# Tile 0's last feed-forward moved under tile 1's expert rows, with each down block as a sum of its own

## The reference, cut to what matters

```python
    u = expert_u[experts]            # (tokens, 8, 16, 1024)
    vsel = expert_v[experts]
    act = gelu(einsum('thkd,td->thk', u, hb))
    x = x + mod5 * einsum('thk,thkd->td', gate * act, vsel)
```

```python
for l in range(2):
    h = rms_norm(x, norm_mix[l])
    x = x + (short_conv_mixer(h) if l == 0 else moba_attention(h, ...))
    x = x + mem_cross_attention(rms_norm(x, ...), memory_l)
    x = x + (silu(g) * u) @ w_down[l]     # g, u = split(rms_norm(x, ...) @ w_gu[l]), 2816 wide each
return rms_norm(x, norm_final)
```

## Time and profile before

| | |
|---|---|
| median of 3 runs | 1847.34 us (1842.53 to 1847.86) |
| the profiled execution's own time | 1849.94 us |
| its span, first to last instruction | 1848.1 us |
| mean granted clock of TensorE | 0.942 of full |
| PE busy, span | 1631.3 us, 88% |
| moved from and to memory | 595.21 MB, 322 GB/s over the span |

### The profile page before, as it was taken

One profiled execution on the slowest core, in us unless ns is written; L12 is line 12 of the kernel. 1 busy time (PEld: TensorE's weight loads), 2 busy tenths in 40 slices (PEclk: granted clock), 3 DMA queues, 4 the chain that ended last, 5 costly groups with the idle time before them and its releaser, 6 DMA issues.

```text
span 1848.1 us, 15547 instructions
## 1 busy us (share of the span) xinstructions
PE 1631.3 (88%) x5460; PEld 760.7 (41%) x5460; DVE 739.3 (40%) x1784; ACT 485.1 (26%) x1267; POOL 284.0 (15%) x268
## 2 busy tenths in 40 slices
PE   6998998497679997987899998889999999988998
PEld 3444464163134542333333333344445444454443
DVE  3653156766594566546544544441101010031000
ACT  3311224322322323324343224232111010122110
POOL 1000002333333333222222223220000000000000
PEclk8998999799789998899999999999999999999999
DMA  9535338999999999999999999977775877654674
GB/s 355 198 144 182 141 136 325 395 388 417 421 386 374 402 421 420 414 421 398 400 397 421 421 420 421 415 321 268 285 284 211 318 289 274 266 222 182 245 300 182
DMA packets 94956, 595.21 MB, mean 322 GB/s; under 512 B 7024, under 2 KB 7024, under 8 KB 28192
## 3 DMA queue, kind: packets, MB, share of 16 engines
q1 hardware_dynamic: 56576, 319.28, 44.2%
q0 software_dynamic: 37584, 270.75, 36.0%
q10 hardware_dynamic: 720, 4.19, 0.6%
HBM read 593.15 MB, written 1.05 MB: 322 GB/s over the span
## 4 chain that ended last, share of the span: by engine, by line
PE 75%; DMA 9%; DVE 8%; ACT 4%; issue 2%; POOL 1%; DVEq 0%; SPq 0%; ACTq 0%; POOLq 0%
PE bank L973 35%; PE bank L1139 9%; PE bank L1052 8%; DMA arena<-in_peer_rows,pidx 7%; PE bank L684 6%; PE bank L946 3%; DVE arena L2063 3%; PE bank L937 2%; DMA ring<-in_w_mod 2%; PE bank L761 2%; PE bank L980 1%; PE bank L738 1%; PE bank L1033 1%; PE bank L781 1%; PE bank L656 1%
## 5 line engine op out<-in xcount | busy, mean ns | idle before, releaser
L1601 POOL DMA_INDIRECT arena<-in_peer_rows,pidx x256 | 279.1, 1090 | 917.6 <-PE bank L1139 596.1
L1139 PE MATMUL bank<-arena,keep 128*32 128x512 f32 x1024 | 279.0, 698 | 124.8 <-ACT keep L1558 124.7
L2063 DVE SCALAR_TENSOR_TENSOR arena<-arena,ring 128x1024 f32<-128x1024 f32 x256 | 305.7, 1223 | 173.0 <-DMA arena<-in_peer_rows,pidx 170.8
L973 PE MATMUL bank<-ring,arena 128*128 128x512 f32 x736 | 322.2, 597 | 9.7 <-ACT arena L1459 7.9
L973 PE MATMUL bank<-ring,hT_all 128*128 128x512 f32 x544 | 241.5, 599 | 4.9 <-DVE hT_all L2120 2.6
L973 PEld LDWEIGHTS bank<-ring,arena 128*128 128x128 f32 x736 | 139.7, 192 | 181.4 <-issue 181.4
L1139 PEld LDWEIGHTS bank<-arena,keep 128*32 128x32 f32 x1024 | 53.0, 120 | 298.0 <-ACT keep L1558 165.7
L973 PEld LDWEIGHTS bank<-ring,hT_all 128*128 128x128 f32 x544 | 102.0, 191 | 136.8 <-issue 136.7
L2170 DVE TENSOR_TENSOR x_all<-x_all,bank 128x512 f32<-128x512 f32 x24 | 16.5, 688 | 228.8 <-PE bank L1052 125.7
L1545 ACT ACTIVATE pf<-pf 128x2 f32<-128x2 f32 x128 | 25.8, 201 | 305.5 <-DVE arena L2063 305.2
L684 PE MATMUL bank<-ring,hT_all 128*128 128x512 f32 x192 | 89.0, 622 | 3.0 <-DVE hT_all L1678 3.0
(11 more groups left out here) (365 smaller groups left out, 1559.0 us busy)
## 6 DMA issues: line engine op xcount, KB each, us to landing
ring<-in_weights SPq DMA_DIRECT2D x126, 2048.0 KB
ring<-in_w_mod SPq DMA_DIRECT2D x12, 2048.0 KB
ring<-in_w_in SPq DMA_DIRECT2D x6, 2048.0 KB
ring<-in_weights SPq DMA_DIRECT2D x8, 1024.0 KB
arena<-in_peer_rows,pidx POOLq DMA_INDIRECT x256
ring<-in_weights SPq DMA_DIRECT2D x8, 512.0 KB
mem_all<-in_b_mod POOLq DMA_DIRECT2D x3, 512.0 KB, 11.0
hT_all<-in_xT ACTq DMA_DIRECT2D x1, 1024.0 KB, 7.3
```

What stands on the lines that cost most here:

```text
L973: m = mm(b[:, :], src[:, k], slot8[w][:, k], start=(k == 0), stop=(k == KC - 1))
L1139: m = mm(acc[b][r:r + 32, :], diag[n % 8], vslot[n % SLOTS][:, b * 512:(b + 1) * 512], start=(n % 128 < 4), stop=(n % 128 >= 124))
L1601: nc.gpsimd.indirect_dma_start(out=row_in[n % SLOTS], out_offset=None, in_=a["peer_rows"], in_offset=bass.IndirectOffsetOnAxis(ap=pidx[:, ...
L2063: stt(uslot[n % SLOTS], uslot[n % SLOTS], 1.0, h2g[n % 4], ALU.mult, ALU.mult, accum_out=pact2[:, 16 * (g % 2) + k:16 * (g % 2) + k + 1]). ...
```

## The change

All of tile 0's steps except `final 0` are placed under the rows; the planner's time for a pick is 5.9 us for 3.7, so that the last step lands at n = 250. `LATE` goes, and `AFTER_ROWS` is `final 0` of tile 0 and then tile 1's steps alone. SP's load order follows, 17 blocks of tile 0's second `gu1` and `dn1` now ahead of tile 1's first. The order of the other steps is the same; their places change. Some of them by n, before and after:

| step | before | after |
|---|---|---|
| turn mem0 / probs0 / values0 | 156 / 166 / 170 | 152 / 160 / 164 |
| turn ffn0 / fturn0 5 / turn blk | 174 / 200 / 212 | 168 / 184 / 192 |
| bprobs / bvalues / turn mem1 | 228 / 232 / 236 | 204 / 208 / 212 |
| probs1 / values1 / mo1 0, 1 | 246 / 250 / 252 | 220 / 224 / 226 |
| turn ffn1 / gu1 0, 1 / dn1 4, 5 | behind the rows | 228 / 230 / 250 |

A down block is now a unit: its contraction starts and ends in its own bank, and VectorE adds it to `x`. This holds for both tiles and layers. Two buffers of tile 0 move: the second layer's attention output and its probabilities.

```diff
-LAYER_FIRST, LAYER_LAST, PICK_US = 136, 252, 3.7
-UNDER_ROWS, LATE = [], []
+LAYER_FIRST, PICK_US = 136, 5.9
+UNDER_ROWS = [_w for _w, _, _ in STEPS]
 _at, _load = LAYER_FIRST, float(LAYER_FIRST)
 for _w, _us, _lag in STEPS:
     _at = max(_at + _lag, 2 * int(_load // 2))
     _load = max(_load, _at) + _us / PICK_US
-    if _at <= LAYER_LAST and not LATE:
-        UNDER_ROWS.append(_w)
+    if _w != "final 0":
+        assert _at < 256
         PICK_WORK.setdefault(_at, []).append("layer 0 " + _w)
-    else:
-        LATE.append((_w, _us))
-AFTER_ROWS = []
-for _w, _us, _lag in STEPS:
-    while _lag and LATE:
-        _late, _late_us = LATE.pop(0)
-        AFTER_ROWS.append((0, _late))
-        if _late_us > 2 and not (_late[:2] == "dn" and _late[-1] not in "25"):
-            break
-    AFTER_ROWS.append((1, _w))
-AFTER_ROWS += [(0, _w) for _w, _ in LATE]
+AFTER_ROWS = [(0, "final 0")] + [(1, _w) for _w, _, _ in STEPS]
...
-                zT=..., cvT=blocks(high), qT=blocks(high), oT=blocks(low),
-                probs=[v.rearrange("p (h n) -> p h n", h=MH) for v in (first, later)], probs_low=work,
+                zT=..., cvT=blocks(high), qT=blocks(high), oT=[blocks(low), blocks(high)],
+                probs=[v.rearrange("p (h n) -> p h n", h=MH) for v in (first, low)], probs_low=work,
...
                 elif kind == "dn":
                     half, c = divmod(int(arg), 3)
-                    if c == 0:
-                        open_unit(f"dn{l}{t}{half}", steps_ahead=True)
-                    b = bank[unit(f"dn{l}{t}{half}") % 4]
                     w = weights(piece[f"dn{l}{t}", int(arg)])
-                    for k in range(8 * c, min(8 * c + 8, FC)):
+                    ks = range(8 * c, min(8 * c + 8, FC))
+                    b = open_unit(f"dn{l}{t}{arg}")
+                    for k in ks:
                         if half == 0 and k % 4 == 0:
                             unit_read(f"ft{l}{t}{k // 4}")
-                        m = mm(b[:, :], v.fT[k], slot8[w][:, k % 8], start=(k == 0), stop=(k == FC - 1))
-                    if c == 2:
-                        open_unit(f"dn{l}{t}{half}", opened_ahead=True)
-                    m.then_inc(unit_ready if c == 2 else sem(f"dn{l}{t}_used"), 1)
+                        m = mm(b[:, :], v.fT[k], slot8[w][:, k % 8], start=(k == ks[0]), stop=(k == ks[-1]))
+                    m.then_inc(unit_ready, 1)
...
-                elif kind in ("cout", "mo", "bo") or kind == "dn" and arg in "25":
-                    half = int(arg) if kind != "dn" else int(arg) // 3
-                    name = {"cout": f"co{t}", "mo": f"lo{l}{t}", "bo": f"bo{t}", "dn": f"dn{l}{t}"}[kind] + str(half)
+                elif kind in ("cout", "mo", "bo", "dn"):
+                    half = int(arg) // (3 if kind == "dn" else 1)
+                    name = {"cout": f"co{t}", "mo": f"lo{l}{t}", "bo": f"bo{t}", "dn": f"dn{l}{t}"}[kind] + arg
                     c = slice(half * 512, (half + 1) * 512)
+                    if kind == "dn" and arg not in "03":
+                        copied(f"dn{l}{t}{int(arg) - 1}")
                     tt(x[:, t, c], x[:, t, c], unit_in(name)[:, :], ALU.add).then_inc(unit_free["D"], 1)
```

More of the change, by code:

```diff
@@ L268, in units_of @@
                  "mo": [("lo{l}{t}{a}", "D")], "gu": [("gu{l}{t}{a}", "D")], "fturn": [("ft{l}{t}{a}", "A")],
-                 "dn": [("dn{l}{t}" + str(int(arg) // 3), "D")] if arg in "25" else [],
[1 row of a table added]
                  "bk": [("bk{t}{a}", "A")], "bq": [("bq{t}{a}", "A")], "bv": [("bv{t}{a}", "A")],
@@ L444, in tile_buffers @@
                 squares=work, hT=blocks(at((hT_all, 1024), (arena, 3072))), kvT=blocks(first), b_tok=low, z_tok=high, q_tok=low,
-                zT=at((h2_all, 0), (arena, 6144), 1040).rearrange("p (k n) -> p k n", k=KC), cvT=blocks(high), qT=blocks(high), oT=blocks(low),
-                probs=[v.rearrange("p (h n) -> p h n", h=MH) for v in (first, later)], probs_low=work,
+                zT=at((h2_all, 0), (arena, 6144), 1040).rearrange("p (k n) -> p k n", k=KC), cvT=blocks(high), qT=blocks(high), oT=[blocks(low), blocks(high)],
+                probs=[v.rearrange("p (h n) -> p h n", h=MH) for v in (first, low)], probs_low=work,
                 pT=work.rearrange("p (h k n) -> p h k n", h=MH, k=2),
@@ L541, in build_program @@
                 last_unit[name, i] = {"cin": "ci", "cout": "co"}.get(step, step) + f"{t}{i}"
[L542 to L545, removed]
+            elif step[:-1] in ("q", "mo", "gu", "dn") and step[-1] in "01":
+                last_unit[name, i] = {"q": "lq", "mo": "lo"}.get(step[:-1], step[:-1]) + f"{step[-1]}{t}{i}"
         def part_read(i):
@@ L563, in wait_released @@
                 eng.wait_ge(unit_ready, unit(last_unit[name, i]) + 1)
-            elif (name, i) in middle:
+            else:
                 eng.wait_ge(sem("piece_used"), middle.index((name, i)) + 1)
-            else:
-                assert name[:2] == "dn"
-                eng.wait_ge(sem(f"{name}_used"), 2 * (i // 3) + i % 3 + 1)
         def tile_x_wait(eng, t, name, u):
@@ L574, in tile_x_wait @@
             else:
-                eng.wait_ge(unit_free["D"], units_freed({"mem0": "co", "ffn0": "lo0", "blk": "dn0", "mem1": "bo", "ffn1": "lo1", "final": "dn1"}[name] + f"{t}{u}", "D"))
+                eng.wait_ge(unit_free["D"], units_freed({"mem0": "co{t}{u}", "ffn0": "lo0{t}{u}", "blk": "dn0{t}{d}", "mem1": "bo{t}{u}", "ffn1": "lo1{t}{u}",
+                                                              "final": "dn1{t}{d}"}[name].format(t=t, u=u, d=3 * u + 2), "D"))
         @block.sync
@@ L1035, in layer_step @@
                 elif kind == "mo":
-                    layer_unit(f"lo{l}{t}{arg}", (f"mo{l}{t}", int(arg)), v.oT, (f"v{l}{t}0", f"v{l}{t}1"))
+                    layer_unit(f"lo{l}{t}{arg}", (f"mo{l}{t}", int(arg)), v.oT[l], (f"v{l}{t}0", f"v{l}{t}1"))
                 elif kind == "gu":
@@ L1498, in layer_step @@
                 elif kind == "values":
-                    unit_copy(f"v{l}{t}1", v.oT[:, 4:8])
+                    unit_copy(f"v{l}{t}1", v.oT[l][:, 4:8])
                 elif kind == "gu":
@@ L2185, in layer_step @@
                 elif kind == "values":
-                    unit_copy(f"v{l}{t}0", v.oT[:, 0:4])
+                    unit_copy(f"v{l}{t}0", v.oT[l][:, 0:4])
                 elif kind == "gu":
```

## The result

The changed kernel takes 1872.37 us in the median (1862.61 to 1873.19, 4 runs) against 1847.33 before: a ratio of 1.0125, 95% interval 1.0102 to 1.0149. It is slower by 25 to 26 us; 17 were forecast, as 1864, with a range of 1836 to 1883.

A forecast was written before the change was run, and what follows sets the result against it. Rows stage before: TensorE and DMA both nearly full, 37 of 53.3 us idle put on VectorE's order. +124.6 under the rows and -107.2 behind give +17.4 on 1847.3: 1864 us, 8 in 10 within 1836 to 1883.

The forecast's parts named there:

- The rows stage: From pair n = 136 to the last pair: grows by 124.6 us as tile 0's last feed-forward moves in.
- the gaps were counted slot by slot: TensorE's waits at ten rows-stage slots, priced from VectorE's evacuation, top-k block and next dots: together 48.3 us.
- The short waits: Rows stage: some ten further TensorE waits of 0.5 to 2 us, together 8.7 us.
- the late-row waits: Rows stage: 16 us of TensorE's idle time before, put on late transfers, goes in the changed kernel.
- The rival that made the change a gain: Rows stage: only transfers count, products fill the gaps, growth is 82.2 us, time down to 1822; chance 0.17.
- Behind the rows: From the last pair to tile 1's feed-forward: 112.8 us for 220.0, a gain of 107.2.
- The first product: Tile 1's convolution start behind the last pair: 9.3 us, waiting for the norm's row, whose load takes 6.9.
- 1.0 for the clock: Behind the rows: 1.0 us added for the clock after the longer gap ahead of tile 1's convolution.
- the memory attention: Tile 1 behind the rows: priced at 44.4 us, turn to turn, from its twin where tile 1 ran alone.
- From tile 1's feed-forward on: The rest of the kernel after tile 1's first steps: nothing changes.
- The partial sums: Down blocks ending in their own banks: 16 more VectorE adds, 11 us, lie under products and cost 0.
- each gap above 3.3 us leaves the next pair slow: Rows stage: the pair after such a gap takes 3.63 us for 1.91; nine for eight, +1 us.

The follow-up runs named there:

- a_again: The changed kernel once more with no edit, on another occasion: 1870.23 us, ratio to before 1.0144.
- a_ahead: The changed kernel with VectorE's dot products taken one pair earlier in its order from n = 136: 1834.65 us, ratio to before 0.9932.
- a_notop: The changed kernel without the top-k blocks of the last six groups of tile 1's picks: 1828.21 us, ratio to before 0.9913.
- a_light: The changed kernel loading only 256 KB of 2 MB of each weight block used under the rows: 1866.16 us, ratio to before 1.0115.
- b_light: The kernel before, loading only 256 KB of 2 MB of each weight block used under the rows: 1821.42 us, ratio 0.9861.
- old_plan: The changed kernel with the step places of before, keeping the separate down blocks and moved buffers: 1845.39 us, ratio to before 0.9990.
- the mixed one: The changed kernel with dots one pair ahead and tile 0's last six down blocks dealt behind the rows: 1821.17 us, ratio to before 0.9869.
- a_ahead4: The changed kernel with dots two pairs ahead and tile 0's final step two places later: 1878.51 us, ratio to before 1.0180.
- b_ahead: The kernel before with VectorE's dot products taken one pair earlier from n = 136: 1843.61 us, ratio 0.9979.

## Why the prediction was right

**The rows stage.** The forecast was +124.6 us; it was +121.7 in the first profile and +124.3 in `a_again`. Of products it had 120.9, measured as 115.9 and 120.2, and of idle time 3.7, measured as 5.9 and 4.1. Inside, the gaps were counted slot by slot, and in the first profile each came within half a microsecond: 160: 7.3, measured 7.00; 192: 5.8 and 5.91; 204: 7.0 and 7.33; 208: 4.9 and 4.48; 220: 6.3 and 5.99; 224: 3.1 and 2.62; 184: 3.7 and 3.88; 152, 168 and 212: 3.4 and 3.36. Sum of the ten 48.3 and 47.3; idle in all 57.0 and 59.2. The short waits were 11.9 us and not 8.7; three were longer than the 2 us I gave them, 2.22 at n = 156, 2.04 at 244 and 2.61 at 252. That the cause is VectorE's order is shown from two sides: `a_ahead` moves the dots and leaves the work, `a_notop` leaves the block out and keeps the order, and both take 34 us off the stage.

**Transfers.** That the late-row waits would go was right (0.8 us left, and `a_light`: no change). Their share in the kernel before was put at 16 us; `b_light` has 21.8, of which 14.4 are idle time (53.3 to 38.9, forecast 37 left) and 7.4 busy time, much of it in products that no longer follow a gap at the lower clock: 32 products at n = 154 took 15.67 us in before and 13.97 in `b_light`. The forecast, +124.6, already took the idle time off. The rival that made the change a gain, stage bound by transfers, is refuted by `a_light`. Its point of decision was well put: gaps below 40 us. `a_ahead` has 32.6 and is faster than before.

**Behind the rows.** The forecast 112.8 us was measured as 112.9 and, in `a_again`, 111.8 (1378.31 to 1490.13), but three of its terms were wrong and cancelled; that the sum fits is luck. The first product came after 6.0 us and not 9.3: I had taken the load's 6.9 us over, and in its new place it took 3.7. The first five blocks took 36.9 us from start to start (1385.97 to 1422.87) and not 34.3, where I had 1.0 for the clock. And the memory attention took 46.0 us (1446.85 to 1492.86) and not its twin's 44.4: its 32 products with the values ran 5.44 us for 3.81.

**Where it was short.** From tile 1's feed-forward on I wrote that nothing changes. It took 378.4 us for 373.7, and 378.2 in `a_again` (1490.13 to 1868.3). 3.4 of it are two starts: the first three blocks after each turn take 22.5 us and not 20.8. Another 1.6 are again 32 products of a memory attention; smaller differences of both signs make the rest. This is the step that was wrong by the most, 4.7 us. The first profile has 3.8 us more ahead of n = 136, which `a_again` doesn't have. Together the spans differ by 23.2 and 20.2 us, where the medians differ by 25 and 26. That difference lies mostly in which executions were profiled: before's was 2.6 us above its median of the first comparison and 5.7 above that of the second, the changed kernel's 0.8 above it and at it.

**The partial sums** were priced at 0, and `old_plan` agrees; the last down projection's 88 products take 37.93 us in before and in the changed kernel.

## What to carry to other kernels

Before moving work under a stage, count that stage's idle time by what ends it, and count it again for the new order: it is not a pool that new work fills, since a gap that comes from one engine's program order stays in place, and moves of the plan can put more of them in. Where a helper engine does side work between the evacuation of one step and what the next one needs, move the needed work ahead of the evacuation. Here one step was right and two were not: the second step was paid for with the depth of the row buffers. And when two plans bracket the balance between engine and transfers, the mixed one is worth a run: here it beat both.

## What the runs showed of the hardware

Two things were not expected. First, the load of the last norm's row, 512 KB, was 6.9 us to landing in the kernel before. The same list of loads, by issue and time to landing, has for the changed kernel:
```profile
arena<-in_norm_final ACTq DMA_DIRECT2D x1, 512.0 KB, 3.7
```
So the time before was no price for it in its new place. It is 6.9 to 7.2 us in the four kernels with before's plan, 3.3 to 3.7 in nine of the ten profiles with a new plan and 5.6 in `a_ahead4`. Beside it the DMA engines moved 311 GB/s in before (1254 to 1262 us) and 133 in the changed kernel (1380 to 1384); no run tells whether that is the reason.

Second, the clock behind one and the same short gap. Tile 1's second feed-forward starts 1.8 to 1.9 us after its turn in every kernel here, with the same instructions. TensorE's timelines of `old_plan` and of the changed kernel, the products with the memory's values and the start of the feed-forward:
```profile
1695.24 3.81 PE L1029 MATMUL bank<-arena,mem_all 128*128 128x128 f32 x32
...
1717.15 20.84 PE L969 MATMUL bank<-ring,arena 128*128 128x512 f32 x48 [1.81 <-ACT arena L1452]
```
```profile
1721.58 5.44 PE L1019 MATMUL bank<-arena,mem_all 128*128 128x128 f32 x32
...
1745.13 22.54 PE L959 MATMUL bank<-ring,arena 128*128 128x512 f32 x48 [1.82 <-ACT arena L1442]
```
The start is 20.84 us in before, `old_plan` and `b_ahead`, in both feed-forwards of tile 1 (the first stands behind a gap of 1.4 us there), and 22.4 to 22.5 in both, in all ten profiles with a new plan; `b_light` has 20.84 in the first and 22.54 in the second. The extra 1.7 us are products at the lower of the two levels. The gaps of the memory attention ahead are the same, but its products are not: their granted clock was 0.69 over the changed kernel's 5.44 us, and 1.00 over before's 3.81. In all 28 starts (two in each of 14 profiles) the slow one follows slowed products (4.8 to 5.4 us) and the fast one full ones (3.7 to 3.8), although in the changed kernel the two blocks between them run at full clock (1.00 from 1727.9 to 1741.7 us). So the difference does not begin at the gap. That the moment in the execution matters is shown in the rows stage: the pair at n = 168, in the changed kernel's first profile and in `a_again`, is the same program behind the same gap.
```profile
904.50 1.91 PE L1122 MATMUL bank<-arena,keep 128*32 128x512 f32 x8 [3.36 <-ACT keep L1541]
```
```profile
900.80 3.63 PE L1122 MATMUL bank<-arena,keep 128*32 128x512 f32 x8 [3.37 <-ACT keep L1541]
```
So the prediction's sentence that each gap above 3.3 us leaves the next pair slow holds in most cases and not in all. Why the starts of tile 1 fall the same way in every kernel with a new plan, no run here tells.
